# Six modulation pieces on GpSimd in place of TensorE, and first-layer products in halves

## The chip, the cores and the metric

The kernel runs on one core of one Trainium2 chip. The metric is the device time of one execution in microseconds; the median over the runs is what counts.

## The reference, cut to what matters

A token matrix x (256 tokens, 1024 features) and a context y (256 tokens) go through two mixing layers, and x then through a block with dilated attention, a convolution and a feed-forward part. The change touches the modulation of the first two layers, which comes from the vectors c and c_ctx alone, and the order of the products `h @ w_in` and of the attention in these layers:

```python
silu_c, silu_cc = jax.nn.silu(c), jax.nn.silu(c_ctx)
for l in range(DEPTH):                       # DEPTH = 2
    shift, scale, gate = jnp.split(silu_c @ w_mod[l] + b_mod[l], 3, axis=-1)
    shift_c, scale_c, gate_c = jnp.split(silu_cc @ w_mod[l] + b_mod[l], 3, axis=-1)
    hx = _rmsnorm(x, norm_g[l]) * (1.0 + scale[:, None, :]) + shift[:, None, :]
    hy = _rmsnorm(y, norm_g[l]) * (1.0 + scale_c) + shift_c
    fy, gy, qy, ky, vy, ay = _branches(hy, ...)   # products with w_in, Fourier, gating, q, k, v
    fx, gx, qx, kx, vx, ax = _branches(hx, ...)
    ox = _blocked_attention(qx, k_all, v_all) * jax.nn.silu(ax)
    x = x + gate[:, None, :] * (jnp.concatenate([fx, gx, ox], axis=-1) @ w_out[l])
```

`w_mod[l]` is 1024 x 3072. The kernel treats it as six pieces of 512 columns each, (l, n) with n = 0, 1 the shift, 2, 3 the scale and 4, 5 the gate.

## The kernel before, in words

Four engines each run a program of their own, written out by hand in the order in which it is carried out; semaphores tie them together, and nothing is scheduled by a planner. A wait blocks all that stands behind it on its engine. `tensor_program`, `scalar_program`, `vector_program` and `sync_program` walk through the same loops, and each must take its part of a step at the place that the others expect. Activations are kept transposed: features on the 128 partitions, tokens in the columns (512 in layer 0, context and x side by side; 256 in layer 1).

**Weights.** SyncE issues the weight chunks in a fixed order (`chunks` in `sync_program`, L2007) into a ring of four slots, `raw`, of 128x1024 each. A chunk may be issued when the chunk four before it has been taken from its slot. Nearly all are split for accuracy: ScalarE writes the rounded part `whi` (`highs`, L898), VectorE the rest `wlo` (`lows`, L1339), and TensorE makes three products per 128 rows, `whi*hh`, `whi*hl`, `wlo*hh` (`lin`, L350 to L355). `highs(key)` and `lows(key)` do not stop at the chunk that `key` needs. They go on to chunks further on, four ahead on ScalarE and three on VectorE, and only the generator `ahead` (L191) ends the run: it stops before a chunk i if one of the chunks from the present one to i - 4 is unsplit. So an engine can come to wait for a chunk that is needed much later.

**Modulation.** The four pieces (0, 2), (0, 0), (0, 3), (0, 1) are made at the start. The other pieces are made beside attention: `mod_g(l, n, g)` (L448) multiplies one unsplit raw chunk (two times 128 rows by 512 columns) with 32 columns of silu(c) on TensorE, four groups to a piece; ScalarE copies the 96x512 sums to `modrow` (`row`, L902), `mod_t` (L459) turns them with four transposes, and `bias` (L1363) on VectorE adds up and adds `b_mod`. In layer 0 the list `MODSTEPS0` gives one such step to each of 30 attention items: six pieces, (0, 4), (0, 5), (1, 2), (1, 3), (1, 0), (1, 1), of four groups and one transpose step each. In layer 1 the pieces (1, 4) and (1, 5) go the same way.

**Layer 0, in order** (`layer(0)`): the six first products (`FIRST`, L506 to L508), in two halves of their 1024 rows; the product for `gv` and the rotary key part (`lin_tm`, L420 to L422); the sums for the norms (L554, L558); k, v and q (L571, L573, L581); the Fourier part (L612 to L633); then attention. On ScalarE the copies out of PSUM after `lin_tm` (L1015) stand behind `highs` of the last chunk of that product. On VectorE the rotary tables (L1472, L1475) and the statistics (L1482 to L1352) stand behind `lows` of the same chunk.

**Attention.** 32 items in layer 0 (16 with 256 keys, 16 with 512), 16 in layer 1. At step i TensorE makes the scores of item i (L666), VectorE their maximum (L1673), ScalarE the exponentials (L1114), VectorE the division (L1680, L1682) of item i - 1, TensorE the transposes (L674) of item i - 2 and the values (L689) of item i - 4. The table `BESIDE` puts whole products between the scores and the transposes of some steps:

```python
BESIDE = ({0: ("agate", 0), 2: ("agate", 1), 4: ("agate", 2), 6: ("agate", 3), 9: ("ggate", 0), 12: ("gu", 0), 15: ("ggate", 1), 18: ("gu", 1), 20: ("gws", 0)},
          {0: ("agate", 0), 1: ("agate", 1), 3: ("agate", 2), 4: ("agate", 3), 6: ("gu", 1), 8: ("gws", 0)})
```

`LATE` says at which step the Fourier and spatial results are made ready for the last product, `wout`. GpSimd has no program: its four instructions are the framework's.

## Time and profile before

| | us |
|---|---|
| median of 3 runs | 981.33 (981.15 to 981.83) |
| the profiled execution, its own time | 986.22 |
| its span | 984.4 |
| mean granted TensorE clock | 0.965 |
| TensorE busy | 910.2 (92% of the span) |
| VectorE busy | 628.2 (64%) |
| ScalarE busy | 430.2 (44%) |
| GpSimd busy | 0.2 |

The span is the time between the first and the last instruction of the profiled execution. That execution was 4.9 us slower than the median of the runs, 1.8 us of it outside the span. A matmul's end is modelled in the profile, so rows of one engine overlap, and the step from one start to the next says more than the length of a row. TensorE's weight loads (PEld) lie beside its matmuls.

### The profile page before, as it was taken

The numbers are of one execution on the slowest core, as the hardware profiler recorded it, in microseconds if no ns is written. First come the engines' busy times: TensorE is split into PE (matmuls) and PEld (weight loads), VectorE is DVE, ScalarE is ACT, GpSimd is POOL, SyncE is SP. The second block draws the span as 40 slices with busy tenths as digits, with TensorE's granted clock in tenths as the row PEclk, the third lists the DMA queues.
The fourth block names the chain that finished last, engine by engine and source line by source line (L and its number), as shares of the span: only waits on it lengthen the run. The fifth ranks groups of instructions, "written<-read, shape, count | busy, mean of one in ns | idle before, by whom it ended". The sixth has DMA issues, their size and how long they took to land.

```text
span 984.4 us, 14348 instructions
## 1 busy us (share of the span) xinstructions
PE 910.2 (92%) x5858; PEld 746.5 (76%) x5858; DVE 628.2 (64%) x1242; ACT 430.2 (44%) x721; POOL 0.2 (0%) x4
## 2 busy tenths in 40 slices
PE   5899999999899799997999999898989799999994
PEld 1577666565478677764998888788888799999993
DVE  3454764644645749656679998976677755555554
ACT  3262143433533345345444444365543644444432
POOL 0000000000000000000000000000000000000000
PEclk9899999999799799999999999999999899999997
DMA  9560133434413133242556665442455256556531
GB/s 356 220 208 1 43 111 103 150 106 155 136 43 104 42 118 129 86 155 93 152 193 185 201 183 159 129 129 66 128 148 174 76 182 192 185 161 209 166 95 43
DMA packets 39954, 135.71 MB, mean 138 GB/s; under 512 B 4432, under 2 KB 5584, under 8 KB 39760
## 3 DMA queue, kind: packets, MB, share of 16 engines
q1 hardware_dynamic: 39024, 130.48, 40.8%
q10 hardware_dynamic: 864, 4.32, 1.2%
q8 instruction: 46, 0.75, 0.3%
q14 instruction: 20, 0.16, 0.1%
HBM read 133.73 MB, written 1.05 MB: 137 GB/s over the span
## 4 chain that ended last, share of the span: by engine, by line
PE 75%; DVE 16%; ACT 5%; DMA 3%; issue 1%; SPq 0%; ACTq 0%; DVEq 0%
PE ps L350 13%; PE ps L351 12%; PE ps L355 11%; PE ps L448 3%; PE ps L422 3%; PE ps L421 3%; PE ps L420 3%; PE ps L666 3%; DVE wlo L1339 3%; PE ps L689 2%; DMA raw<-wpack 2%; DVE AF L1800 2%; PE ps L353 2%; PE ps L868 1%; PE ps L506 1%; PE ps L674 1%
## 5 line engine op out<-in xcount | busy, mean ns | idle before, releaser
L350 PE MATMUL ps<-hh,whi 128*128 128x256 f32 (+1 forms) x1032 | 310.6, 301 | 3.7 <-DVE AF L1845 2.6
L351 PE MATMUL ps<-hl,whi 128*128 128x256 f32 (+1 forms) x1032 | 305.5, 296 | 0.0
L1339 DVE TENSOR_TENSOR wlo<-raw,whi 128x1024 fp32r<-128x1024 f32 (+3 forms) x206 | 234.1, 1150 | 62.7 <-ACT whi L898 62.5
L898 ACT ACTIVATE whi<-raw 128x1024 fp32r<-128x1024 f32 (+3 forms) x206 | 205.0, 997 | 151.2 <-DMA raw<-wpack 70.4
L355 PE MATMUL ps<-hh,wlo 128*128 128x256 f32 (+1 forms) x897 | 265.6, 296 | 0.0
L350 PEld LDWEIGHTS ps<-hh,whi 128*128 128x128 f32 x1032 | 198.9, 193 | 15.3 <-issue 9.0
L351 PEld LDWEIGHTS ps<-hl,whi 128*128 128x128 f32 x1032 | 199.1, 193 | 5.0 <-issue 0.7
L355 PEld LDWEIGHTS ps<-hh,wlo 128*128 128x128 f32 x897 | 173.1, 193 | 4.0
L420 PE MATMUL ps<-whi,hh 128*128 128x512 f32 (+1 forms) x192 | 70.7, 368 | 0.8 <-ACT wk L998 0.8
L421 PE MATMUL ps<-wlo,hh 128*128 128x512 f32 (+1 forms) x192 | 70.2, 366 | 0.0
L422 PE MATMUL ps<-whi,hl 128*128 128x512 f32 (+1 forms) x192 | 70.2, 366 | 0.0
L1114 ACT ACTIVATE AF<-ps,AF 128x512 f32<-128x512 f32 (+1 forms) x48 | 29.6, 617 | 86.9 <-DVE AF L1673 86.9
L1673 DVE TENSOR_REDUCE AF<-ps 128x1 f32<-128x512 f32 (+1 forms) x48 | 28.7, 598 | 37.0 <-PE ps L666 36.7
L1800 DVE SCALAR_TENSOR_TENSOR AF<-AF,cst 128x256 f32<-128x256 f32 x120 | 52.0, 483 | 0.4
L674 PEld LDWEIGHTS ps<-cst,AF 128*128 128x128 f32 x160 | 18.5, 147 | 42.2 <-DVE AF L1682 23.1
L666 PE MATMUL ps<-AF 96*128 96x512 f32 (+1 forms) x96 | 46.9, 571 | 2.3 <-DVE AF L1555 1.3
L420 PEld LDWEIGHTS ps<-whi,hh 128*128 128x128 f32 x192 | 36.0, 188 | 6.6 <-DVE wlo L1339 1.0
L422 PEld LDWEIGHTS ps<-whi,hl 128*128 128x128 f32 x192 | 36.0, 188 | 5.6
L421 PEld LDWEIGHTS ps<-wlo,hh 128*128 128x128 f32 x192 | 36.1, 188 | 5.5
L353 PE MATMUL ps<-hh,wlo 128*128 128x256 f32 (+1 forms) x135 | 39.7, 294 | 0.0
L1971 DVE TENSOR_TENSOR AF<-AF,ps 128x256 f32<-128x256 f32 x22 | 9.3, 421 | 46.9 <-PE ps L353 46.9
L674 PE MATMUL ps<-cst,AF 128*128 128x128 f32 x160 | 28.7, 296 | 11.3 <-DVE AF L1682 11.3
(254 smaller groups left out, 1275.9 us busy)
## 6 DMA issues: line engine op xcount, KB each, us to landing
raw<-wpack SPq DMA_DIRECT2D x196, 512.0 KB, 4.1
AF<-wmod SPq DMA_DIRECT2D x16, 512.0 KB, 10.3
raw<-wpack SPq DMA_DIRECT2D x16, 448.0 KB, 4.1
raw<-wpack SPq DMA_DIRECT2D x24, 256.0 KB, 2.8
XT<-xin SPq DMA_DIRECT2D x4, 512.0 KB, 6.1
raw<-wpack SPq DMA_DIRECT2D x4, 432.0 KB, 3.3
uq<-wuq ACTq DMA_DIRECT2D x2, 768.0 KB, 5.1
cst<-cpack ACTq DMA_DIRECT2D x1, 1093.0 KB, 7.9
```

The lines of the kernel that those rows point to most:

```text
L350: e.matmul(o, wh[:, b], xh(k), start=j == 0, stop=False, skip_group_check=True)
L351: e.matmul(o, wh[:, b], xl(k), start=False, stop=False, skip_group_check=True)
L353: e.matmul(o, wl[:, b], xh(k), start=False, stop=True, skip_group_check=True).then_inc(*M.up(key))
L355: e.matmul(o, wl[:, b], xh(k), start=False, stop=False, skip_group_check=True)
L420: e.matmul(o, xh(k)[:, ts], wh[:, b], start=k == 0, stop=False, skip_group_check=True)
L421: e.matmul(o, xh(k)[:, ts], wl[:, b], start=False, stop=False, skip_group_check=True)
L422: i = e.matmul(o, xl(k)[:, ts], wh[:, b], start=False, stop=k == KD - 1, skip_group_check=True)
L666: e.matmul(ps.ap(key, n), g.Q[0:96, t % 2, h, :], g.K[0:96, h, 0:n], start=True, stop=True, skip_group_check=True).then_inc(*M.up(key))
L674: n = e.transpose(ps.ap(key, P, j * P), g.Pb[:, o:o + P], C("ident"))
L898: e.activation(W.hi(i), W.raw(i), ACT.Copy).then_inc(*HI.up(j))
L1339: e.tensor_tensor(W.lo(i), W.raw(i), W.hi(i), ALU.subtract).then_inc(*LO.up(j))
L1800: e.scalar_tensor_tensor(out=g.CV[:, m, :], in0=g.U[:, m, j:j + 256], scalar=w, in1=g.CV[:, m, :], op0=ALU.mult, op1=ALU.add).then_inc(*V. ...
```

## The change

GpSimd gets a program, `gpsimd_program`. For each of the six pieces and each of the eight blocks k of 128 rows it takes a 128x512 block of `w_mod`, multiplies it by the two per-partition scalars silu(c_ctx)[k] and silu(c)[k], and adds both products to an accumulator of 128x1024. The first block of a piece has the two multiplications alone. That makes 48 block steps: 6 of two instructions and 42 of four. TensorE only sums the accumulator over the partitions, with eight matmuls against one column of ones (`mod_sum`), and `bias` reads that result with one instruction less. The four groups, the copy to `modrow` and the transposes of these six pieces are gone, and with them 24 unsplit chunks of the ring.

The blocks come by DMAs of 256 KB. The first 24 (`MFIRST`) are issued by SyncE, between the weight chunks, into three slots inside the tile `ag`; each from the fourth on waits until GpSimd is done with the block three before it. The other 24 are issued by ScalarE during attention (`MLOAD`), into the places of `modrow` and `ckv`. The sums stand at these places: (0, 4) before the product for `gv`, (0, 5) after the norm sums, (1, 2) before the second `kv_proj`, (1, 3) and (1, 0) at attention steps 13 and 24, (1, 1) before the seventh `wout` product. ScalarE's `agate` tanhs wait for GpSimd, since they write `ag`.

The products beside attention are split into two halves of 512 rows (`lin_first`, `lin_rest`), at two steps each, in both layers, and `LATE` moves from (22, 10) to (27, 14).

```diff
-MODS0 = ((0, 4), (0, 5), (1, 2), (1, 3), (1, 0), (1, 1))
+MODS = ((0, 4), (0, 5), (1, 2), (1, 3), (1, 0), (1, 1))
+MFIRST = 24
+MLOAD = {4 * n // 3: MFIRST + n for n in range(24)}
+MODS_AT = {13: (1, 3), 24: (1, 0)}
-LATE = (22, 10)
+LATE = (27, 14)
+BESIDE = (halves(*(("agate", m, 2 * m, 2 * m + 1) for m in range(4)), ("ggate", 0, 9, 11), ("gu", 0, 13, 15), ("ggate", 1, 17, 19), ("gu", 1, 21, 23), ("gws", 0, 25, 25)),
+          halves(*(("agate", m, 2 * m, 2 * m + 1) for m in range(4)), ("gu", 1, 9, 11), ("gws", 0, 12, 12)))
...
+    def mod_sum(l, n):
+        key = ("modT", l, n)
+        pe.wait_ge(G["mod", l, n], *ps.take(key))
+        acc = K.macc(MODS.index((l, n)))
+        for j in range(4):
+            for s in range(2):
+                i = e.matmul(ps.ap(key, 1, 2 * j + s), acc[:, 512 * s + P * j:512 * s + P * j + P], C("ones", 0, 1), start=True, stop=True, skip_group_check=True)
+        i.then_inc(*M.up(key))
...
+        def mod_load(j):
+            ac.wait_ge(G["w", j - 2] if j >= MFIRST + 2 else M["modT", 0, 1], M[l, "v", 3])
+            e.dma_start(K.mslot(j), K.wmodg[j]).then_inc(*K.mw_in[3 + j % 2].up(("in", j)))
...
+    def mods(a, b):
+        for j in range(a, b):
+            sp.wait_ge(G["w", j - 3] if j >= 3 else K.mm["mod", 0, 2])
+            e.dma_start(K.mslot(j), K.wmodg[j]).then_inc(*K.mw_in[j % 3].up(("in", j)))
...
-    chunks(6, len(W.plan))
+    chunks(6, 9)
+    mods(0, 3)
+    for i in range(6):
+        chunks(9 + i, 10 + i)
+        mods(3 + i, 4 + i)
+    mods(9, 11)
+    chunks(15, 16)
+    mods(11, 17)
+    chunks(16, 17)
+    mods(17, MFIRST)
+    chunks(17, len(W.plan))
...
+def gpsimd_program(K, e):
...
+    for p, a in enumerate(MODS):
...
+        for k in range(KD):
...
+            if k == 0:
+                e.tensor_scalar(o0, w, c0, None, ALU.mult, ALU.bypass).then_inc(*G.up(("p0", j)))
+                e.tensor_scalar(o1, w, c1, None, ALU.mult, ALU.bypass).then_inc(*G.up(("w", j)))
+            else:
+                e.tensor_scalar(tmp, w, c0, None, ALU.mult, ALU.bypass).then_inc(*G.up(("p0", j)))
+                e.tensor_scalar(w, w, c1, None, ALU.mult, ALU.bypass).then_inc(*G.up(("p1", j)))
+                po.wait_ge(G["p0", j])
+                e.tensor_tensor(o0, o0, tmp, ALU.add).then_inc(*G.up(("s0", j)))
+                po.wait_ge(G["p1", j])
+                e.tensor_tensor(o1, o1, w, ALU.add).then_inc(*G.up(("w", j)))
```

Three places show how the change moves instructions. The first is SyncE's queue, from the last early modulation load on, before the change (L2007 is a weight chunk; the rows are chunks 6 to 11, 12 and 13, 14, 15, and from 16 on):

```order
L1997 DMA AF<-wmod 128x1024 x4
L2007 DMA raw<-wpack 128x512 x6
L2007 DMA raw<-wpack 128x864 x2
L2007 DMA raw<-wpack 128x576
L2007 DMA raw<-wpack 128x512
L2007 DMA raw<-wpack 128x1024 x26
```

and with the change (L2064 is a weight chunk, L2071 a block for GpSimd), from chunk 13 on:

```order
L2064 DMA raw<-wpack 128x864
L2071 DMA AF<-wmodg 128x512
L2064 DMA raw<-wpack 128x576
L2071 DMA AF<-wmodg 128x512 x3
L2064 DMA raw<-wpack 128x512
L2071 DMA AF<-wmodg 128x512 x6
L2064 DMA raw<-wpack 128x1024
L2071 DMA AF<-wmodg 128x512 x7
L2064 DMA raw<-wpack 128x1024 x8
```

Chunk 16 (the second `fgate`) now stands behind blocks 11 to 16, and chunk 17 (`agate` 0), 18 and 19 behind blocks 17 to 23, the last of which waits for GpSimd's block step 20.

The second place is ScalarE around the copies after the `gv` product (L1015 before, L1050 now). Before:

```order
L898 ACTIVATE whi<-raw 128x1024 [waits raw_in0]
L974 ACTIVATE AF<-ps 128x512 [waits mm_done]
L898 ACTIVATE whi<-raw 128x1024 [waits raw_in2]
L1015 ACTIVATE AF<-ps 128x32 [waits mm_done]
L1016 ACTIVATE AF<-ps 128x256
```

and with the change:

```order
L933 ACTIVATE whi<-raw 128x1024 [waits raw_in0]
L1009 ACTIVATE AF<-ps 128x512 [waits mm_done]
L933 ACTIVATE whi<-raw 128x1024 [waits raw_in1]
L933 ACTIVATE whi<-raw 128x1024 [waits mm_done,raw_in2]
L1050 ACTIVATE AF<-ps 128x32 [waits mm_done]
L1051 ACTIVATE AF<-ps 128x256
```

Ahead of the copies stood chunks 16 and 18 (`fgate` 1 and `agate` 0), and chunk 17 was an unsplit modulation chunk. Now chunks 16, 17 and 18 stand there: `fgate` 1, `agate` 0 and `agate` 1.

The third is VectorE at the same point, ahead of the rotary tables (L1472 before, L1520 now). Before:

```order
L1339 TENSOR_TENSOR wlo<-raw,whi 128x576 [waits w_high]
L1339 TENSOR_TENSOR wlo<-raw,whi 128x1024 [waits w_high] x2
L1472 TENSOR_TENSOR rtab<-cst 128x64 [waits c1_in]
L1475 TENSOR_TENSOR rtab<-cst 128x2x8 x4
```

and with the change:

```order
L1382 TENSOR_TENSOR wlo<-raw,whi 128x576 [waits w_high]
L1382 TENSOR_TENSOR wlo<-raw,whi 128x1024 [waits w_high] x3
L1520 TENSOR_TENSOR rtab<-cst 128x64 [waits c1_in]
L1523 TENSOR_TENSOR rtab<-cst 128x2x8 x4
L1520 TENSOR_TENSOR rtab<-cst 128x64
L1523 TENSOR_TENSOR rtab<-cst 128x2x8 x4
L1413 TENSOR_TENSOR mod<-ps,cst 128x8 [waits mm_done]
L1532 TENSOR_SCALAR AF<-ps 128x4 [waits mm_done]
```

The splits of chunks 16, 17 and 18 now come ahead of the tables, of the bias of piece (0, 4) (L1413) and of the norm statistics (L1532).

## Rows read from the trace of the kernel before

**Rows 1.** The page, part 1: busy time, share of the span, instructions.

```profile
span 984.4 us, 14348 instructions
...
PE 910.2 (92%) x5858; PEld 746.5 (76%) x5858; DVE 628.2 (64%) x1242; ACT 430.2 (44%) x721; POOL 0.2 (0%) x4
```

**Rows 2.** Stretch: length, busy (x) of PE, PEld, DVE, ACT, POOL; clock; DMA.

```profile
128.00:276.00 148.00, 137.59 (x728) 82.94 (x728) 79.72 (x192) 63.52 (x136) 0.00 (x0) 0.95 0.39 127
```

**Rows 3.** Who waited for whom, 128 to 276 us: in total, times, longest.

```profile
PEld ps L674 <- DVE AF L1682: 14.3, 10, 3.4
```

**Rows 4.** Chain that ended last: start us, length us, what.

```profile
85.93 1.68 PE ps L554 x16
87.61 0.89 PE ps L558 x8
...
227.21 0.98 PE ps L448 x4
```

**Rows 5.** TensorE in order of time, 229 us: start, length, instruction.

```profile
229.48 0.49 PE L459 MATMUL ps<-cst,modrow 96*128 96x96 f32 x4
229.81 0.60 PE L674 MATMUL ps<-cst,AF 128*128 128x128 f32 x4
```

**Rows 6.** SyncE's queue, 49 to 52 us: start, length, DMA.

```profile
50.95 0.33 SPq L2007 DMA_DIRECT2D raw<-wpack  x1
```

**Rows 7.** The page, part 6: DMA issues, KB each, us to landing.

```profile
raw<-wpack SPq DMA_DIRECT2D x196, 512.0 KB, 4.1
...
raw<-wpack SPq DMA_DIRECT2D x24, 256.0 KB, 2.8
```

**Rows 8.** VectorE by line and shape, 128 to 276 us: busy, mean ns.

```profile
L1339 DVE TENSOR_TENSOR wlo<-raw,whi 128x1024 fp32r<-128x1024 f32 x10 | 12.2, 1225 | 21.0 <-ACT whi L898 21.0
...
L1682 DVE TENSOR_SCALAR AF<-AF 128x512 f32<-128x512 f32 x16 | 7.8, 487 | 0.6
```

**Rows 9.** Busy time by stretch, 54 to 90 us: VectorE's line L1339, then L1429.

```profile
54.00:90.00 36.00, 8.78 (x10) 0.99 0.40 136
...
54.00:90.00 36.00, 2.92 (x7) 0.99 0.40 136
```

**Rows 10.** GpSimd in order of time: the last of its four.

```profile
0.33 0.10 POOL L2171 MEMSET const-uint8-127<- 128x1 uint8 x1
```

**Rows 11.** ScalarE in order of time, 60 to 88 us.

```profile
74.75 1.06 ACT L898 ACTIVATE whi<-raw 128x1024 fp32r<-128x1024 f32 x1 [0.87 <-DMA raw<-wpack]
85.97 0.20 ACT L1015 ACTIVATE AF<-ps 128x32 f32<-128x32 f32 x1 [10.16 <-PE ps L422]
```

**Rows 12.** VectorE in order of time, 60 to 91 us.

```profile
76.98 0.22 DVE L1472 TENSOR_TENSOR rtab<-cst 128x64 f32<-128x64 f32 x1
...
77.59 0.43 DVE L1475 TENSOR_TENSOR rtab<-cst 128x16 f32<-128x16 f32 x4
88.54 0.16 DVE L1482 TENSOR_SCALAR AF<-ps 128x4 f32<-128x4 f32 x1 [10.52 <-PE ps L558]
...
90.01 0.17 DVE L1352 SCALAR_TENSOR_TENSOR AF<-AF 128x8 f32<-128x8 f32 x1
```

**Rows 13.** VectorE in order of time, 110 to 116 us.

```profile
112.93 2.48 DVE L1515 COPY AF<-ps 128x512 f32<-128x512 f32 x4
```

**Rows 14.** TensorE in order of time, 88 to 116 us.

```profile
88.36 1.10 PE L571 MATMUL ps<-AF 128*128 128x512 f32 x2
...
114.83 0.59 PE L632 MATMUL ps<-cst,AF 128*128 128x256 f32 x2
```

**Rows 15.** TensorE in order of time, 260 to 276 us.

```profile
260.32 1.11 PE L674 MATMUL ps<-cst,AF 128*128 128x128 f32 x4 [2.49 <-DVE AF L1682]
262.06 1.97 PE L689 MATMUL ps<-AF 128*64 128x128 f32 x16 [0.63 <-ACT AF L1121]
...
273.75 0.66 PE L674 MATMUL ps<-cst,AF 128*128 128x128 f32 x4 [0.94 <-DVE AF L1682]
274.45 1.09 PE L689 MATMUL ps<-AF 128*64 128x128 f32 x16
```

More of the change, by code:

```diff
@@ L298, in mod_order, with halves @@
     return out
[L301 to L303 removed]
+LATE = (27, 14)
 def out_step(l, t):
     return max(8 * (t - 2 * l) + 10, LATE[l] + 2 + t % 2)
[L312 to L313 removed]
+def halves(*places):
+    out = {}
+    for nm, m, a, b in places:
+        out[a] = (nm, m, 0)
+        out[b] = (nm, m, 1)
+    return out
+BESIDE = (halves(*(("agate", m, 2 * m, 2 * m + 1) for m in range(4)), ("ggate", 0, 9, 11), ("gu", 0, 13, 15), ("ggate", 1, 17, 19), ("gu", 1, 21, 23), ("gws", 0, 25, 25)),
+          halves(*(("agate", m, 2 * m, 2 * m + 1) for m in range(4)), ("gu", 1, 9, 11), ("gws", 0, 12, 12)))
 def fills(i):
@@ L544, in layer @@
             lin_many([spec("cq", 0), spec("cq", 1), spec("ckv", 0, True), spec("fin", 0), spec("fin", 1)], ht)
+        if l == 0:
+            mod_sum(0, 4)
         st = (l, "st")
@@ L560, in layer @@
         ps.drop(st)
+        if l == 0:
+            mod_sum(0, 5)
         if l == 1:
@@ L643, in layer @@
                 heads_T("q", 0, 1, y)
+            mod_sum(1, 2)
             kv_proj(1)
@@ L697, in layer @@
         mt = lambda k: V[l, "mix", k]
-        steps = list(MODSTEPS0) if l == 0 else mod_order(((1, 4), (1, 5)))
+        steps = mod_order(MODS1) if l else []
+        half = None
         for i in range(ni + 3):
@@ L711, in layer @@
                 heads_T("q", 1, 0, 1)
+            if l == 0 and i in MODS_AT:
+                mod_sum(*MODS_AT[i])
             if steps:
@@ L731, in layer @@
         for m in range(len(begun), KD):
+            if l == 0 and m == 6:
+                mod_sum(1, 1)
             lin((l, "wout", m), "w_out", l, (P * m, P), range(KD), xh, xl, N, mt)
@@ L980, in gate @@
             highs(key)
-            ac.wait_ge(M[key], *bar)
+            ac.wait_ge(M[key], G["w", min(MFIRST - 3 + m, MFIRST - 1)] if l == 0 and nm == "agate" else None, *bar)
             e.activation(dst, ps.ap(key, N), ACT.Tanh, scale=0.5).then_inc(*A.up(key))
@@ L1132, in layer @@
                 exps(i)
-            if i - 1 in BESIDE[l]:
-                beside(*BESIDE[l][i - 1])
+            if l == 0 and i in MLOAD:
+                mod_load(MLOAD[i])
+            if i - 1 in BESIDE[l] and (BESIDE[l][i - 1][2] or BESIDE[l][i - 1][0] == "gws"):
+                beside(*BESIDE[l][i - 1][:2])
             if l == 0 and i == 0:
@@ L1156, in layer @@
             if i in BESIDE[l] and BESIDE[l][i][0] != "gws":
-                highs((l, *BESIDE[l][i]))
+                highs((l, *BESIDE[l][i][:2]))
             for m in range(2):
@@ L1477, in layer @@
         V.mark((l, "tab"))
+        if l == 0:
+            bias(0, 4)
         st = ps.ap((l, "st"), 8)
@@ L1486, in layer @@
         V.mark((l, "stat"))
+        if l == 0:
+            bias(0, 5)
         n = 4 * len(tiles)
@@ L1619, in layer @@
                 heads_T("q", 0, 1, y)
+            bias(1, 2)
             kv_take(1, 0, M[l, "kT", 0, 1, 4])
@@ L1694, in layer @@
         ni = len(items)
-        steps = list(MODSTEPS0) if l == 0 else mod_order(((1, 4), (1, 5)))
+        steps = mod_order(MODS1) if l else []
         def mod_step(what, a, g_):
@@ L1707, in layer @@
                 norm(i - 1)
-            if i - 1 in BESIDE[l]:
-                beside(*BESIDE[l][i - 1])
+            if i - 1 in BESIDE[l] and (BESIDE[l][i - 1][2] or BESIDE[l][i - 1][0] == "gws"):
+                beside(*BESIDE[l][i - 1][:2])
             if l == 0:
@@ L1738, in layer @@
                     heads_T("q", 1, 0, 1, M[l, "s", 15])
+            if l == 0 and i in MODS_AT:
+                bias(*MODS_AT[i])
             if steps:
@@ L1743, in layer @@
             if i in BESIDE[l] and BESIDE[l][i][0] != "gws":
-                lows((l, *BESIDE[l][i]))
+                lows((l, *BESIDE[l][i][:2]))
             for m in range(2):
@@ L1759, in layer @@
             key = (l, "wout", m)
+            if l == 0 and m == 6:
+                bias(1, 1)
             lows(key, 4 if l == 0 and m == KD - 1 else 3)
@@ L2114, in _ @@
             vector_program(K, e)
+        @block.gpsimd
+        def _(e):
+            gpsimd_program(K, e)
     return plan
```

81 lines of the change are left out of this document (55 added, 26 removed).

## The prediction

> **What bounds the kernel now.** I read the page's first part, then stretches, waits, the chain, and last the order of single instructions. The page shows TensorE busy for 92% of the span and GpSimd with nothing to do [rows 1]. That alone would make any work moved from TensorE to GpSimd a gain. The stretch of layer 0's attention says the same: from 128 to 276 us TensorE is busy for 137.6 of 148 us, VectorE for 79.7 and ScalarE for 63.5, at a granted clock of 0.95 [rows 2]. The largest true wait of TensorE there is for VectorE's divisions, 14.3 us of idle weight loads [rows 3], most of it after 245 us. So before that point a microsecond taken off TensorE is a microsecond of the kernel.
>
> **What leaves TensorE.** A modulation group is one link of 0.98 us in the chain [rows 4]; 24 of them go: 23.5 us. Four transposes hold TensorE for 0.33 us, from 229.48 to the next start at 229.81 [rows 5]; six sets go: 2.0 us. Together 25.5 us.
>
> **What comes to TensorE.** `mod_sum` is eight matmuls of a 128x128 operand on one column. The norm sums have just this form: eight of them took 1.68 us [rows 4]. Six sums are 10.1 us. Two of them, (0, 4) and (0, 5), stand before or inside the wait that I find below and cost nothing; that cover goes if the wait goes, and they then cost 3.4 us. The other four cost 6.7 us. Net on TensorE: 25.5 - 6.7 = 18.8 us gained. The halves issue the same matmuls, and the ring has lost the 24 modulation chunks, so I count the split, `LATE` and the 12 fewer small VectorE and ScalarE instructions at nothing. What hides them is TensorE's own full queue up to 245 us; if VectorE became late there, they would show.
>
> **What GpSimd takes.** Its only rows are 128x1 memsets of 0.10 us [rows 10], so the price of its instructions is not in the trace, and I bound it by VectorE's. VectorE takes 0.49 us for 128x512 with one input, and 1.22 us for 128x1024 with two [rows 8]. Low end: GpSimd is as fast as VectorE, 0.49 us for the multiplication and 0.69 for the addition (the 128x512 splits: nearly all of the ten in 54 to 90 us are of that kind or in proportion, 8.8 us [rows 9]). A full block step is then 2.36 us. High end: 0.69 for the multiplication and 1.22 for the addition, so 3.82 us. I take 0.59 and 1.22, a step of 3.62 us, near the high end, since nothing shows GpSimd to keep VectorE's pace. A first step of a piece, two multiplications, is 1.18 us. The Trainium skill (GPSIMD Engine Reference, "Elementwise — side-by-side cycle accounting") gives 4497 ns for an fp32 `tensor_tensor` of 2048 columns and 1.03 cycles per element at 1.2 GHz for short bodies: an estimate by it is about 1.1 and 0.45 us, a step of 3.1 us, and with that the sum below would be 9 us lower. No row here shows it.
>
> **When GpSimd gets where.** Blocks 0 to 2 are loaded early. Block 3 is issued behind weight chunk 9, which leaves at 50.95 us [rows 6]; 0.33 us more for the issue and 2.8 us for 256 KB [rows 7] put it in place at 54.1 us. From there GpSimd has no gap, for three slots and two steps of 3.62 us cover a landing. It ends block 15 at 54.1 + 12 x 3.62 + 1.18 = 98.7, and block 20 at 98.7 + 1.18 + 4 x 3.62 = 114.4 us.
>
> **The wait that the change adds.** This is the term that decides. SyncE issues chunk 17 only behind block 23, and block 23 waits for GpSimd's block 20: 114.4 us. Behind that chunk hang two queues that need something else. ScalarE rounds chunks 17 and 18 before its copies out of PSUM, and VectorE splits both before the tables, the statistics and all that follows; this is the look-ahead of `highs` and `lows`, which the unsplit chunk 17 used to keep shorter. Before, ScalarE had its last chunk of that group at 74.75 us and waited for TensorE until 85.97, with ten microseconds to spare [rows 11]. Now: 0.7 us for two issues, 4.1 us for 512 KB [rows 7], two roundings of 1.06 us [rows 11], one split of 1.22 us [rows 8], tables of 1.0 us (76.98 to 78.0), a bias of 0.2, and statistics of 1.6 us (88.54 to 90.18) [rows 12]. That is 10.9 us, and the statistics are ready at 125.3 instead of 90.2 us: 35.1 us late. TensorE cannot run on meanwhile: k, v and q are scaled by these statistics, and PSUM banks are full of what ScalarE has not fetched. Further down VectorE's chain reached its Fourier copies at 112.93 and TensorE wanted the first at 114.83 [rows 13, 14]; the first of four copies in 2.48 us ends at 113.5, so 1.3 us of the delay is lost in that gap. The shift at the start of attention is 33.8 us. GpSimd's block 15 (98.7) and block 23 (125.3) are then no wait of their own.
>
> **The clock.** After an idle of 2.5 us at 260 us, four transposes took 1.11 us instead of 0.66 and a set of values 1.97 instead of 1.09 [rows 15]: the granted clock had fallen to its lower level, 1.2 GHz. An idle of 25 us should do the same. I take 3 us for it, some seven microseconds of work at 1.75 times its length; the ends are 0 and 6.
>
> **Sum.** 33.8 + 3 - 18.8 = 18.0 us slower. The profiled execution took 986.2 us, 4.9 more than the median of 981.3. 986.2 + 18.0 = 1004.2, and on the scale of the median 999.3 us.
>
> **Bounds of the forecast.** With the low step of 2.36 us block 20 ends at 93.8, the shift is 13.2, and the sum is -2.6 us (978.7 on the median's scale). With the high step block 20 ends at 118.0, the shift is 37.4 and the sum 21.6 us. With a step from 3.1, the middle of the two ends, to 3.82 us and the clock's ends, the forecast's own range is 988 to 1006.
>
> **Rival one: the two engines hold each other up.** VectorE and GpSimd both read and write SBUF, and nothing in a trace without GpSimd work tells what that costs. At the far end each waits for the other. From 54 to 90 us VectorE has 11.7 us of instructions with two SBUF inputs, ten of L1339 and seven of L1429 [rows 9], nearly all before 78 us, while GpSimd works on blocks 3 to 9. If they exclude each other, block 20 comes 12 us later, at 126. Then blocks 21 to 23 still run (12 instructions) beside VectorE's chain of small ones, and each can hold one up by up to its own 0.6 to 1.2 us: I take 8 us. In attention a division that waits for half an instruction of GpSimd costs some 0.4 us wherever TensorE waits for it, the last dozen items: 5 us. Together 25 us on top: 1024 us. For it speaks that both take 128-partition operands from one memory; against it, that VectorE's splits, run beside a ScalarE busy for 43% of that stretch, keep a mean of 1225 ns [rows 2, 8]. The Trainium skill (SBUF — State Buffer, "Who interferes with whom") has this as a rule: VectorE in a two-port mode or with two SBUF inputs, and GpSimd, take one pair of ports as an exclusive lock. No row here can show it.
>
> **Rival two: faster.** If GpSimd keeps VectorE's pace, block 20 ends at 94, chunk 17 lands at 98, and the shift of 13.2 us is less than the 18.8 us gained. The point from which this decides is a shift of 16 us, block 20 before 97 us, a step below 2.5 us. It gives 975 to 980 us; with the clock at no cost, 976.
>
> **Rival three: the gain in attention is not there.** Without the groups, attention may run at the pace of VectorE and ScalarE, which already hold TensorE up late in it [rows 3], or ScalarE may wait for GpSimd ahead of a load and hold back the exponentials. The groups after 245 us and a wait at some of the 22 such loads would take back 6 to 10 us: 1005 to 1009.
>
> **How the numbers follow.** The forecast has 0.5, the mutual hold 0.29, the fast GpSimd 0.12, the lost gain 0.09. A measurement of this kernel can tell about 0.2%, 2 us, from no change. All but the fast GpSimd are slower; of that case I give 0.09 to faster and 0.03 to no change, and 0.02 of the forecast's low edge goes to no change. The range takes in both ends of the step and the mutual hold: 978 to 1024. The predicted time is 999.
>
> **What would show it.** Right: GpSimd's starts repeat about every 3.6 us; ScalarE waits some 35 us for chunk 17 (raw) before its copies at L1050, and VectorE about as long at L1382 ahead of the tables; TensorE is idle between about 90 and 121 us; attention of layer 0 lasts about 126 instead of 148 us. Wrong: chunk 17 lands before 100 us, or TensorE has no gap over 10 us there. Mutual hold would show in VectorE's 128x512 splits longer than 0.69 us between 54 and 62 us.

## The result and the profile after: 1071 us against 981

The changed kernel takes 1071.2 us (median of 4 runs, 1071.2 to 1073.4), the kernel before 981.2 beside it. The ratio is 1.092, 95% interval 1.090 to 1.094. The forecast was 999, its range ended at 1024. The sign and the mechanism were right, the size was not.

The page's first part of the kernel after, to be held against [rows 1]:

```profile
PE 909.4 (85%) x5834; PEld 765.0 (71%) x5834; DVE 658.1 (61%) x1236; ACT 427.5 (40%) x715; POOL 273.9 (26%) x184
```

TensorE has as much to do as before, in a longer span. GpSimd works for 274 us. VectorE has six instructions fewer and 30 us more: they got longer.

The stretches of the kernel after (columns as in [rows 2]):

```profile
54.00:90.00 36.00, 22.55 (x85) 17.81 (x84) 11.03 (x12) 9.71 (x18) 35.83 (x24) 0.76 0.43 138
90.00:128.00 38.00, 17.34 (x123) 17.25 (x122) 2.00 (x1) 1.54 (x2) 38.00 (x29) 0.68 0.21 63
128.00:175.00 47.00, 13.40 (x33) 7.76 (x34) 14.38 (x30) 7.04 (x14) 43.13 (x31) 0.53 0.19 56
209.00:357.00 148.00, 119.84 (x613) 86.17 (x611) 89.96 (x172) 52.93 (x118) 128.42 (x82) 0.86 0.23 72
```

From 54 to 171 us GpSimd alone is full. The three other engines are each busy for less than half of 54 to 175 us (TensorE 53.3 of 121), and the granted clock falls to 0.53. The last line is layer 0's attention over the same length as in [rows 2]: TensorE is busy for 120 of 148 us instead of 138.

SyncE's issues in time (start, length, line). L2064 issues weight chunks, L2071 blocks; a long row is a series whose waits lie in it:

```profile
90.18 28.11 SPq L2071 DMA_DIRECT2D AF<-wmodg  x6
118.34 0.43 SPq L2064 DMA_DIRECT2D raw<-wpack  x1
123.50 31.38 SPq L2071 DMA_DIRECT2D AF<-wmodg  x7
154.92 112.06 SPq L2064 DMA_DIRECT2D raw<-wpack  x12
```

Chunk 16 leaves at 118.34 and chunk 17 at 154.92, behind GpSimd's blocks 13 and 20. The two queues of the prediction hang on them. ScalarE and VectorE in the same stretch (in brackets the idle time before, and what ended it):

```profile
122.12 1.06 ACT L933 ACTIVATE whi<-raw 128x1024 fp32r<-128x1024 f32 x1 [44.04 <-DMA raw<-wpack]
158.68 1.06 ACT L933 ACTIVATE whi<-raw 128x1024 fp32r<-128x1024 f32 x1 [35.01 <-DMA raw<-wpack]
```

```profile
123.21 2.00 DVE L1382 TENSOR_TENSOR wlo<-raw,whi 128x1024 fp32r<-128x1024 f32 x1 [44.57 <-ACT whi L933]
159.76 3.67 DVE L1382 TENSOR_TENSOR wlo<-raw,whi 128x1024 fp32r<-128x1024 f32 x2 [34.55 <-ACT whi L933]
168.84 1.28 DVE L1395 SCALAR_TENSOR_TENSOR AF<-AF 128x8 f32<-128x8 f32 x1
170.12 1.20 DVE L1545 TENSOR_REDUCE AF<-AF 128x16 f32<-128x1024 f32 x1
```

The statistics end at 170.1; in the kernel before they ended at 90.2 [rows 12]. Attention starts at 209.0, before at 128.7. TensorE's rows there:

```profile
86.93 3.57 PE L488 MATMUL ps<-cst,AF 128*128 128x1 f32 x16 [9.58 <-POOL AF L2124]
129.15 3.57 PE L488 MATMUL ps<-cst,AF 128*128 128x1 f32 x16 [21.81 <-POOL AF L2124]
167.08 2.07 PE L600 MATMUL ps<-AF 128*128 128x512 f32 x2 [32.45 <-DVE mod L1413]
208.96 0.60 PE L694 MATMUL ps<-AF 96*128 96x256 f32 x2
```

Behind these idles a piece's sum takes 3.57 us; the granted clock over both rows is 0.50. The sum of (1, 1), later on, is a row of 1.84 at full clock (the norm sums, of the same form, count 1.68 in the chain [rows 4]):

```profile
400.19 1.84 PE L488 MATMUL ps<-cst,AF 128*128 128x1 f32 x16
```

The sign that the prediction named for a mutual hold, a 128x512 split longer than 0.69 us between 54 and 62 us, is there:

```profile
55.20 1.77 DVE L1382 TENSOR_TENSOR wlo<-raw,whi 128x512 fp32r<-128x512 f32 x1
```

What GpSimd costs: one of its groups (busy us, mean ns of one), then one step, block 21, in time:

```profile
L2120 POOL TENSOR_SCALAR AF<-AF,c 128x512 f32<-128x512 f32 x33 | 58.5, 1773 | 0.0
```

```profile
154.48 1.58 POOL L2119 TENSOR_SCALAR AF<-AF,c 128x512 f32<-128x512 f32 x1
156.02 1.58 POOL L2120 TENSOR_SCALAR AF<-AF,c 128x512 f32<-128x512 f32 x1
157.55 1.28 POOL L2122 TENSOR_TENSOR AF<-AF 128x512 f32<-128x512 f32 x1
158.77 1.29 POOL L2124 TENSOR_TENSOR AF<-AF 128x512 f32<-128x512 f32 x1
160.02 1.59 POOL L2119 TENSOR_SCALAR AF<-AF,c 128x512 f32<-128x512 f32 x1
```

With VectorE idle a block step is 160.02 - 154.48 = 5.54 us. The prediction took 3.62 and ended its range at 3.82. The product with one input is the dearer of the two: 1.54 us from start to start against 1.23.

### The profile page after: what moved, and what is told of

Read it like the earlier page. It is cut to its first block, busy times and chain, and to the rows that moved or that the text cites. A ratio compares the mean times of both kernels' runs of the same rounds, so it can differ in the third digit from the quotient of the medians.

```text
span 1071.5 us, 14537 instructions
## 1 busy us (share of the span) xinstructions
PE 909.4 (85%) x5834; PEld 765.0 (71%) x5834; DVE 658.1 (61%) x1236; ACT 427.5 (40%) x715; POOL 273.9 (26%) x184
## 4 chain that ended last, share of the span: by engine, by line
PE 62%; POOL 14%; DVE 14%; issue 4%; ACT 3%; DMA 3%; SPq 0%; ACTq 0%; DVEq 0%; POOLq 0%
PE ps L363 10%; PE ps L364 10%; PE ps L368 9%; POOL AF L2120 4%; POOL AF L2122 3%; POOL AF L2119 3%; PE ps L433 3%; PE ps L435 3%; PE ps L434 3%; DVE wlo L1382 2%; POOL acc L2119 2%; DVE AF L1857 2%; PE ps L608 1%; PE ps L366 1%; PE ps L618 1%
## 5 line engine op out<-in xcount | busy, mean ns | idle before, releaser
L1382 DVE TENSOR_TENSOR wlo<-raw,whi 128x1024 fp32r<-128x1024 f32 (+3 forms) x206 | 238.9, 1174 | 122.2 <-ACT whi L933 121.9
L363 PE MATMUL ps<-hh,whi 128*128 128x256 f32 (+1 forms) x928 | 271.3, 292 | 3.7 <-DVE AF L1902 2.6
L364 PE MATMUL ps<-hl,whi 128*128 128x256 f32 (+1 forms) x928 | 267.6, 288 | 0.0
L368 PE MATMUL ps<-hh,wlo 128*128 128x256 f32 (+1 forms) x806 | 232.5, 288 | 0.0
L363 PEld LDWEIGHTS ps<-hh,whi 128*128 128x128 f32 x928 | 177.8, 192 | 9.2 <-issue 5.1
L364 PEld LDWEIGHTS ps<-hl,whi 128*128 128x128 f32 x928 | 177.8, 192 | 2.6 <-issue 0.7
L368 PEld LDWEIGHTS ps<-hh,wlo 128*128 128x128 f32 x806 | 154.4, 192 | 1.7
L2120 POOL TENSOR_SCALAR AF<-AF,c 128x512 f32<-128x512 f32 x33 | 58.5, 1773 | 0.0
L702 PEld LDWEIGHTS ps<-cst,AF 128*128 128x128 f32 x160 | 20.9, 156 | 45.8 <-DVE AF L1735 34.1
L694 PE MATMUL ps<-AF 96*128 96x512 f32 (+1 forms) x96 | 47.7, 580 | 0.9 <-ACT AF L1081 0.9
L2124 POOL TENSOR_TENSOR AF<-AF 128x512 f32<-128x512 f32 x33 | 44.1, 1336 | 0.0
L488 PE MATMUL ps<-cst,AF 128*128 128x1 f32 x96 | 16.1, 297 | 31.4 <-POOL AF L2124 31.4
```

The source lines that it names most:

```text
L363: e.matmul(o, wh[:, b], xh(k), start=j == 0, stop=False, skip_group_check=True)
L364: e.matmul(o, wh[:, b], xl(k), start=False, stop=False, skip_group_check=True)
L368: e.matmul(o, wl[:, b], xh(k), start=False, stop=False, skip_group_check=True)
L702: n = e.transpose(ps.ap(key, P, j * P), g.Pb[:, o:o + P], C("ident"))
L1382: e.tensor_tensor(W.lo(i), W.raw(i), W.hi(i), ALU.subtract).then_inc(*LO.up(j))
L2120: e.tensor_scalar(w, w, c1, None, ALU.mult, ALU.bypass).then_inc(*G.up(("p1", j)))
```

## The experiments

All times are medians; each is compared with the kernel before in the same batch (978.5 to 981.3 us, single runs of it 974 to 986). The last two columns are read from TensorE's rows of the one profiled execution: the start of layer 0's first score matmul (L666 in before and e5 to e7, L676 in e4, L694 in the others), and the time from there to the start of the scores of that layer's last item.

| Kernel | us | ratio to before [95%] | first score at | first to last |
|---|---|---|---|---|
| before | 981.2 | 1 | 128.7 | 142.6 |
| after | 1071.2 | 1.092 [1.090, 1.094] | 209.0 | 146.0 |
| e1 all steps narrow | 976.1 | 0.996 [0.993, 0.998] | 138.5 | 121.6 |
| e2 chunks first | 1047.7 | 1.068 [1.065, 1.072] | 184.5 | 143.9 |
| e3 products whole | 1063.4 | 1.085 [1.081, 1.088] | 210.2 | 136.9 |
| e4 halves alone, on before | 984.2 | 1.004 [1.001, 1.006] | 130.4 | 145.0 |
| e5 before, GpSimd multiplies beside it | 1020.6 | 1.043 [1.037, 1.049] | 158.4 | 148.1 |
| e6 before, GpSimd memsets beside it | 979.9 | 1.000 [0.996, 1.004] | 126.1 | 142.2 |
| e7 before, four GpSimd forms beside it | 996.7 | 1.018 [1.008, 1.027] | 142.6 | 141.4 |
| e8 narrow ahead of attention | 1000.1 | 1.021 [1.015, 1.027] | 136.9 | 142.7 |
| e9 e8 and GpSimd's own loads | 1006.4 | 1.026 [1.019, 1.033] | 140.1 | 147.8 |
| e10 products in the two-input form | 1056.5 | 1.078 [1.073, 1.083] | 195.9 | 143.5 |
| e11 all of GpSimd's cost away | 969.2 | 0.989 [0.985, 0.993] | 135.3 | 121.7 |
| e12 e8 with memsets in attention | 982.5 | 1.002 [0.999, 1.005] | 139.6 | 128.5 |
| e13 memsets in all steps | 1041.7 | 1.062 [1.058, 1.066] | 195.6 | 125.9 |
| e14 three mends together | 1038.9 | 1.059 [1.056, 1.063] | 185.2 | 137.5 |

### Is it GpSimd's time at all? (e1)

```diff
+                n_ = slice(0, 16)
-                e.tensor_scalar(tmp, w, c0, None, ALU.mult, ALU.bypass).then_inc(*G.up(("p0", j)))
+                e.tensor_scalar(tmp[:, n_], w[:, n_], c0, None, ALU.mult, ALU.bypass).then_inc(*G.up(("p0", j)))
...
```

> Of the changed kernel's block steps after the first of each piece, GpSimd computes only 16 of the 512 columns; every instruction, wait, DMA and sum stays, so the modulation is wrong and only GpSimd's own time is taken out. Theory (the loss is GpSimd's pace, handed on by waits): GpSimd is never late, chunk 17 lands before 80 us, and the time is that of before less what TensorE was relieved of: 981 - 25.5 + 10.1, that is 964 to 970. Rival (the loss lies in the order, the halves, the DMAs or the extra waits themselves): over 990.

976.1 us: with GpSimd's long steps gone, 95 us go, five more than the change had cost. So the loss is GpSimd's time. The result is 6 us above the expected band. Chunk 17 did not land before 80 us as expected: it is issued at 87.82, still behind all 24 blocks. Attention starts 9.8 us later than in the kernel before and is 21.0 us shorter from first to last score.

### The order of the chunks (e2), the halves (e3, e4)

```diff
-    mods(9, 11)
-    chunks(15, 16)
-    mods(11, 17)
-    chunks(16, 17)
-    mods(17, MFIRST)
-    chunks(17, len(W.plan))
+    chunks(15, 19)
+    mods(9, MFIRST)
+    chunks(19, len(W.plan))
```

> The changed kernel with SyncE's queue reordered alone: weight chunks 15 to 18 are issued ahead of blocks 9 to 23, so neither look-ahead waits for GpSimd. Theory: the 34.5 us in which ScalarE and VectorE wait for chunk 17 go, but TensorE then stands at its own wait for the sum (0, 5), block 15, until 129 us, and for (1, 2), block 23, until about 171 us; attention starts near 176 instead of 209, and the time is 1071 - 33 = 1038, within 8. Rival (chunk 17 is the only cause): a shift near zero, time under 1000. Rival (mutual hold is the cause): no change, 1065 to 1072.

1047.7, 24 us less than the changed kernel, 1.7 above the expected band. Attention starts at 184.5, where 176 was expected. The wait for chunk 17 is gone, and the sum of piece (0, 5) is late next; TensorE's row of it in e2:

```profile
131.52 3.57 PE L488 MATMUL ps<-cst,AF 128*128 128x1 f32 x16 [21.36 <-POOL AF L2121]
```

```diff
-    BESIDE: every product of attention in halves, LATE = (27, 14)
+    BESIDE: whole products at the steps of the kernel before, LATE = (22, 10)
```

> The changed kernel with the products beside attention whole again, at the steps of before, and LATE as before; GpSimd as in the change. Theory (halves are worth nothing while GpSimd sets the pace): 1066 to 1076. Rival (the halves carry part of the loss through PSUM or weight loads): under 1062.

> The kernel before with the halves and LATE of the change alone, no GpSimd. Theory: same matmuls, TensorE full: within 2 us of 981. Rival (halves smooth attention): 974 to 979. Rival (halves cost): over 984.

In the changed kernel the halves with their `LATE` cost 8 us (1071.2 to 1063.4), between the two expectations; alone on the kernel before they cost about 3 us (ratio 1.004), at the edge of "halves cost". The prediction had counted them at nothing. The gain of e3 lies in attention, 136.9 us against 146.0. Split and `LATE` were not separated.

### The mutual hold by itself (e5, e6, e7)

```diff
+        @block.gpsimd
+        def _(e):
...
+            for i in range(420):
+                e.wait_ge(sg, n)
+                e.tensor_tensor(a, a, b, ALU.mult).then_inc(sg, 1)
+                n += 1
```

> The kernel before, and on GpSimd 420 two-input multiplications of 128x244 in a scratch of its own, one behind the other, for which nobody waits. Work and output are the reference's. Theory of the mutual hold (VectorE and GpSimd hold each other up where both read and write the on-chip memory): VectorE's rows between 20 and 300 us get longer, the 128x512 splits (0.49 and 0.69 us alone) by at least half on the mean, and the kernel by 10 to 50 us though nobody waits for GpSimd. Rival (the two don't touch; what was held up in the changed kernel was held by its own waits): VectorE's rows keep their lengths within 5%, and the time is 981 within 3 us.

> As the run with the two-input multiplications, but with 420 memsets of 128x244, which write and read nothing. If the mutual hold comes of GpSimd's reading, this kernel takes 981 within 3 us with VectorE's rows unchanged; if any GpSimd work holds VectorE, it is as slow per GpSimd operation as the run with the multiplications.

Nobody waits for GpSimd in either. The multiplications cost 42 us, the memsets nothing. The multiplications run until 382 us, the shorter memsets only until 155. VectorE's groups of the kernel before, of e5 and of e6, over the whole span, but L1429 from 50 to 128 us:

```profile
L1682 DVE TENSOR_SCALAR AF<-AF 128x512 f32<-128x512 f32 x32 | 15.6, 487 | 1.1
L1339 DVE TENSOR_TENSOR wlo<-raw,whi 128x512 fp32r<-128x512 f32 x20 | 13.6, 688 | 1.3 <-ACT whi L898 1.2
L1429 DVE SCALAR_TENSOR_TENSOR hl<-AF,mod,hh 128x256 fp32r<-128x256 f32 x8 | 3.5, 482 | 0.0
```

```profile
L1682 DVE TENSOR_SCALAR AF<-AF 128x512 f32<-128x512 f32 x32 | 19.6, 612 | 1.1
L1339 DVE TENSOR_TENSOR wlo<-raw,whi 128x512 fp32r<-128x512 f32 x20 | 18.6, 936 | 1.4 <-ACT whi L898 1.4
L1673 DVE TENSOR_REDUCE AF<-ps 128x1 f32<-128x512 f32 x32 | 21.9, 686 | 19.3 <-PE ps L666 19.3
...
L1429 DVE SCALAR_TENSOR_TENSOR hl<-AF,mod,hh 128x256 fp32r<-128x256 f32 x8 | 7.0, 914 | 0.0
```

```profile
L1339 DVE TENSOR_TENSOR wlo<-raw,whi 128x512 fp32r<-128x512 f32 x20 | 13.6, 687 | 3.3 <-ACT whi L898 3.2
...
L1429 DVE SCALAR_TENSOR_TENSOR hl<-AF,mod,hh 128x256 fp32r<-128x256 f32 x8 | 3.5, 479 | 0.0
```

Beside the multiplications VectorE's instructions with two on-chip inputs take 914 instead of 482 ns. The means over the whole span hide a part of it. Between 20 and 320 us the 128x512 splits take 1103 instead of 689 ns, and the fast one-input division (L1682) 737 instead of 487. The reduction that reads PSUM keeps 686 ns. In e6 all the 128x512 divisions come after the last memset and say nothing; five 128x256 divisions came before it and took 435 ns on the mean instead of 354. The Trainium skill (SBUF — State Buffer, "Who interferes with whom") has this as an exclusive lock between GpSimd and VectorE in a two-port mode, or with two SBUF inputs. With two inputs, it says, VectorE contends only with a GpSimd instruction that reads SBUF. The rows agree: beside memsets the two-input splits keep 687 ns. Most of the 42 us come ahead of attention (158.4 against 128.7).

The pace of each form was e7's question:

> The kernel before, and on GpSimd ten rounds of ten memsets, ten one-input products by an immediate number, ten one-input products by a number for each partition, and ten two-input products, all 128x244 in a scratch of its own, for which nobody waits. It is for the pace of each form. Theory (the number for each partition makes the one-input form slow): immediate 0.35 us and per-partition 0.8 us start to start. Rival one (the one-input form is slow in both): both 0.75 to 0.85 us, above the two-input form at 0.6 to 0.7. Rival two (1.54 us of the changed kernel was contention with VectorE): both one-input forms under the two-input form where VectorE is idle.

Shortest, median and longest of 100 each, all 128x244 (memset; immediate; per-partition number; two-input):

```profile
L2125 POOL MEMSET gx<- x100: 301/301/544, 4.0 to 306.4; 128x244 f32 x100
L2129 POOL TENSOR_SCALAR gx<-gx x100: 817/819/2056, 7.8 to 317.2; 128x244 f32<-128x244 f32 x100
L2133 POOL TENSOR_SCALAR gx<-gx,c x100: 892/894/2498, 16.8 to 330.1; 128x244 f32<-128x244 f32 x100
L2137 POOL TENSOR_TENSOR gx<-gx x100: 697/709/1769, 26.8 to 340.6; 128x244 f32<-128x244 f32 x100
```

Rival one: the one-input form is slow with either number, already in the shortest rows, so it is no contention. These are lengths of rows; each instruction waits for the one before, and from start to start they repeat every 0.36, 0.90, 0.99 and 0.79 us.

### A cheaper product (e10)

```diff
-            c0, c1 = K.c32[:, 32 * k:32 * k + 1], K.c32[:, 32 * k + 1:32 * k + 2]
+            c0, c1 = (K.c32[:, 32 * k + s:32 * k + s + 1].broadcast_to([P, 512]) for s in range(2))
-                e.tensor_scalar(tmp, w, c0, None, ALU.mult, ALU.bypass).then_inc(*G.up(("p0", j)))
+                e.tensor_tensor(tmp, w, c0, ALU.mult).then_inc(*G.up(("p0", j)))
...
```

> The changed kernel with GpSimd's products written in the two-input form (the number for each partition read again and again as second operand): a block step should take four times 1.27 instead of twice 1.57 and twice 1.27 us, 0.6 less, and the result is the same. If the time ahead of attention is GpSimd's 20 blocks one behind the other, statistics and attention come 11 to 14 us earlier, and with a little of the same in attention the kernel takes 1050 to 1060. Rival (GpSimd's price was not what set the place of attention, but the hold-ups beside VectorE and the order of the chunks): 1066 or more. Rival two (the repeated operand costs GpSimd as much or more): 1071 or above.

1056.5, in the band. The product with a repeated operand costs less than guessed; block 9 of e10:

```profile
86.20 1.04 POOL L2119 TENSOR_TENSOR AF<-AF,c 128x512 f32<-128x512 f32 x1
...
88.20 1.28 POOL L2122 TENSOR_TENSOR AF<-AF 128x512 f32<-128x512 f32 x1
89.44 1.28 POOL L2124 TENSOR_TENSOR AF<-AF 128x512 f32<-128x512 f32 x1
90.68 1.04 POOL L2119 TENSOR_TENSOR AF<-AF,c 128x512 f32<-128x512 f32 x1
```

A step is 4.48 us. Attention starts 13.1 us earlier and the kernel is 14.7 shorter, so the time does go by GpSimd's steps ahead of attention.

### What GpSimd costs in attention (e8, e9, e12, e13)

```diff
-                n_ = slice(0, 16)
+                n_ = slice(0, 16 if first else 512)
```

> The changed kernel in which the steps of blocks 0 to 23 (before attention) behind the first of each piece compute 16 of 512 columns, and those of blocks 24 to 47 (in attention) all 512: the modulation of the first three pieces is wrong. Theory (80 us of the loss come ahead of attention and some 10 to 17 in it, where ScalarE's loads wait for GpSimd): attention starts at 138 us as with all steps narrow (976.1 us), and the kernel takes 986 to 995. Rival (the pace in attention hardly matters, since the loads wait only because everything is late): 976 to 979. Rival two (attention is paced by GpSimd's 24 blocks of 5.5 us and loses more once it starts early): 1000 or more.

1000.1, 5 us above the theory's band and at the very edge of rival two's: the wide steps of attention cost 24 us once everything else is early (e1 to e8). Two causes were left: ScalarE's exponentials behind its waits for GpSimd, or the mutual hold. First the loads were taken off ScalarE:

```diff
-            if l == 0 and i in MLOAD:
-                mod_load(MLOAD[i])
...
+            for jj in ((MFIRST, MFIRST + 1) if j == MFIRST else (j + 1,) if j > MFIRST and j + 1 < 2 * MFIRST else ()):
+                po.wait_ge(G["w", jj - 2] if jj >= MFIRST + 2 else M["modT", 0, 1], M[0, "v", 3])
+                e.dma_start(K.mslot(jj), K.wmodg[jj]).then_inc(*K.mw_in[3 + jj % 2].up(("in", jj)))
```

> The changed kernel with the steps of blocks 0 to 23 narrow (as in the run at 1000 us), in which GpSimd itself issues the loads of blocks 24 to 47, each as its slot comes free, and ScalarE none: ScalarE's exponentials no longer stand behind a wait for GpSimd (16.5 us in 6 waits there between 128 and 300 us). The modulation of the first three pieces is wrong. Theory A (of the 24 us that the wide steps in attention cost, most is ScalarE's waiting for GpSimd): 978 to 986. Theory B (most is the mutual hold of VectorE and GpSimd, which stays): 988 to 1002, with VectorE's 128x512 splits in attention still near 0.78 us instead of 0.49.

1006.4, above both bands: nothing won. But VectorE's sixteen 128x512 divisions were at 1163 ns there, longer than in e8 (841), and each load was a new GpSimd row of 0.59 us, so a second thing had changed and the run does not settle it. The next one does:

```diff
-                e.tensor_scalar(tmp, w, c0, None, ALU.mult, ALU.bypass).then_inc(*G.up(("p0", j)))
...
+                for dst, key in ((tmp, "p0"), (w, "p1"), (o0, "s0"), (o1, "w")):
+                    n = 3 if key == "p0" else 2
+                    for r in range(n):
+                        po.wait_ge(G.now())
+                        e.memset(dst, 1.0).then_inc(*G.up((key, j)) if r == n - 1 else G.up())
```

> The changed kernel with the steps of blocks 0 to 23 narrow, as in the run at 1000 us, and in blocks 24 to 47 the four operations of a step replaced by nine memsets of 128x512 (one at about 0.6 us, worked out from 0.30 us for 128x244): GpSimd is as long at each block, ScalarE's loads wait for it as before, but GpSimd reads nothing. The modulation is wrong. Theory (the 24 us of the wide steps in attention are the mutual hold): 976 to 982. Rival (they are ScalarE's waiting for GpSimd, and the run with GpSimd's own loads lost what it gained there through its DMA issues): 992 or more. Between: both.

982.5, half a microsecond above the theory's band. With GpSimd nearly as long at each block and ScalarE still waiting for it (14.3 us in 5 waits, 16.5 in 6 in e8), but nothing read, 18 of the 24 us are gone. From first to last score attention takes 128.5 us instead of 142.7. VectorE from 128 to 300 us, in e12 and then in e8:

```profile
L1382 DVE TENSOR_TENSOR wlo<-raw,whi 128x1024 fp32r<-128x1024 f32 x12 | 14.5, 1216 | 2.0 <-ACT whi L933 2.0
L1735 DVE TENSOR_SCALAR AF<-AF 128x512 f32<-128x512 f32 x16 | 10.8, 676 | 0.6
L1643 DVE TENSOR_TENSOR AF<-AF,rtab 128x64 f32<-128x64 f32 x16 | 2.5, 219 | 0.0
```

```profile
L1382 DVE TENSOR_TENSOR wlo<-raw,whi 128x1024 fp32r<-128x1024 f32 x10 | 13.4, 1349 | 1.4 <-ACT whi L933 1.4
L1735 DVE TENSOR_SCALAR AF<-AF 128x512 f32<-128x512 f32 x16 | 13.4, 841 | 0.6
L1643 DVE TENSOR_TENSOR AF<-AF,rtab 128x64 f32<-128x64 f32 x16 | 7.7, 542 | 0.0
```

The two-input instructions are free of the memsets: the rotations (L1643) take 219 ns beside them and 542 beside the readings. The division is not free: 676 ns for 128x512 (516 in e1) and 505 for 128x256 (355 in e1; 371 in e8). Over all 32 divisions memsets cost nearly as much as readings, 18.9 us of busy time against 19.3, and 13.9 in e1. So the 18 us do not come from the division. VectorE's instructions in that attention add up to 86.0 us in e1, 90.9 in e12 and 104.7 in e8, and nearly all of the 13.8 between the last two lie in two-input instructions, 5.2 of them in the rotations. The splits count for little: of the eight in e8 between 128 and 276 us seven took 1.22 us and one 2.28. e12 is no exact price, since it still has some hold and its steps are a little shorter.

The same memsets in every step of the changed kernel:

> The changed kernel with nine memsets in the place of the four operations in every step behind the first of a piece, ahead of attention too: GpSimd's pace of about 5.5 us a block is kept, its reading is gone. The modulation is wrong. Theory (ahead of attention the 80 us are pace and order alone, in attention the mutual hold costs 10 to 20): attention starts at 200 to 209 us instead of 209, and the kernel takes 1042 to 1060. Rival (the mutual hold is a large part ahead of attention too): attention starts ahead of 195 us and the time is under 1040. Rival two (no hold matters anywhere): 1066 or more.

1041.7, 29.5 less than the changed kernel, just under the theory's band and above the rival's. Attention starts at 195.6, between theory and rival, and takes 125.9 us instead of 146.0. Some 4 us of these 13.4 are the memsets' slightly quicker step (37.04 us for seven of them, 5.29 each), the rest is put down to time in which GpSimd and VectorE held each other; one execution shows it.

### All of the gain, and all mends

e11 takes narrow steps, whole products and the chunk order of e2 together; its diff is theirs.

> All of GpSimd's cost taken away, the whole gain left: steps behind the first of each piece narrow (modulation wrong), the first layers' products whole at the places of the kernel before, chunks 15 to 18 issued ahead of blocks 9 to 23. TensorE does the reference's work without the modulation's six pieces. The prediction's term for this was a gain of 18.8 us: 962 against 981. Theory (the term was right and only the price of GpSimd wrong): 960 to 967. Rival (TensorE's 25.5 us were largely cover for its waits for VectorE and ScalarE, which come out as idle time): 970 to 978.

969.2, 2.2 us above the first band and 0.8 below the rival's. From first to last score attention is 20.9 us shorter than before, and it begins 6.6 us later. Three of the six sums now stand ahead of it, rows of 1.84, 2.58 and 1.84 us, which is nearly all of that.

e14 has the chunk order of e2, the whole products of e3 and the product form of e10, and computes all of it.

> The changed kernel with three mends together: products whole at the places of the kernel before (8 us alone), chunks 15 to 18 issued ahead of blocks 9 to 23 (24 us alone), GpSimd's products in the two-input form (15 us alone). The work and the output are the reference's. If the mends add up, 1024 (1018 to 1032), still slower than the kernel before. Rival (with the chunks first GpSimd is no longer ahead of anything until its second sum, and the mends overlap): 1033 to 1045. Rival two (the rest falls away once GpSimd is in time): under 1000.

1038.9, the first rival: the mends do not add up. Attention starts at 185.2, no earlier than with the chunks alone. The sum of (0, 5) comes 10.4 us earlier than in e2 (121.15 against 131.52), and VectorE's chain of small dependent instructions behind it gives the time back. It runs while GpSimd still works (piece (1, 2), until about 157.5 us). Rows of e14:

```profile
154.19 0.97 DVE L1393 TENSOR_TENSOR AF<-AF 128x16 f32<-128x16 f32 x1
...
162.23 0.17 DVE L1393 TENSOR_TENSOR AF<-AF 128x16 f32<-128x16 f32 x1
```

The same instruction takes 0.97 us beside GpSimd and 0.17 us without: each waits out about one instruction of GpSimd. But in e2 the same chain ran beside a working GpSimd too, and it was mostly quick. Two rows of VectorE and one of GpSimd from e2:

```profile
154.63 0.17 DVE L1393 SCALAR_TENSOR_TENSOR AF<-AF 128x16 f32<-128x16 f32 x1
154.84 0.47 DVE L1395 SCALAR_TENSOR_TENSOR AF<-AF 128x16 f32<-128x16 f32 x1
```

```profile
154.59 1.57 POOL L2117 TENSOR_SCALAR AF<-AF,c 128x512 f32<-128x512 f32 x1
```

The difference lies, by these rows, in the form of GpSimd's products; no run took it by itself. Of VectorE's small instructions (up to 16 columns) with two on-chip inputs that started under a GpSimd `tensor_tensor`, 30 of 34 took over 0.3 us in e14; under a `tensor_scalar` it was 8 of 39 in e2. A `tensor_scalar` holds them only in its first 0.7 us: the second row ends 0.72 us after the product began, and three more in e2 end 0.70 to 0.71 after theirs. So the cheaper two-input product of e10 is also the one that holds VectorE all the time. TensorE pays for it with this wait in e14, which is 4.86 us in e2:

```profile
166.62 1.22 PE L659 MATMUL ps<-cst,AF 128*128 128x256 f32 x2 [15.35 <-DVE AF L1569]
```

No version that computes everything came below the kernel before. By these runs none with a smaller share on GpSimd should: a piece saves at most 20.9 / 6 = 3.5 us, and three pieces in attention cost 24 us, 8 each. That is worked out, not run.

## Why the prediction was wrong in size

**What bounds the kernel, and what leaves TensorE: right.** The prediction had attention at 126 instead of 148 us. Without GpSimd's cost it is 20.9 us shorter (e11). Over the whole kernel the forecast's gain was 18.8 us, or 15.4 with the two early sums paid for, as in e11; e11 has 1.1% (0.7 to 1.5), about 11, since attention begins 6.6 us later. The price of a sum holds at full clock.

**The wait that the change adds: right in its place.** Chunk 17 is issued behind block 20, ScalarE waits 35.0 us for it, VectorE 34.6, and the statistics are late. What stands in front of it was overlooked: chunk 16 behind block 13, with a wait of 44.0 us of its own. It comes ahead of chunk 17 and adds nothing to the sum.

**The step that failed is "What GpSimd takes": 3.62 us for a block step, high end 3.82.** It was 5.53. The bound came from VectorE, on the reasoning that the high end was already VectorE's 1024-column time for a GpSimd addition of 512 columns. For the addition that was right (1.22 taken, 1.23 measured). The product was taken at 0.59 and measured at 1.54, 2.6 times as long; one input was assumed cheaper than two, as on VectorE, and on GpSimd it is dearer. The estimate by the Trainium skill (GPSIMD Engine Reference, "Elementwise — side-by-side cycle accounting"), 0.45 us, was further off; for the addition its 1.1 us is near the 1.23 measured. Between block 3 and the end of block 20 lie 16 full and 2 first steps: 16 x 1.91 + 2 x 1.90 = 34.4 us more than forecast. Another 3.9 went by up to the issue of chunk 17, 3.5 of it in which GpSimd was held up or idle. Block 3 began 2.3 late, and behind block 20 came 15.2 us instead of 10.9 up to the statistics, since VectorE's splits, tables and small instructions there were themselves held (rows at 159.76 and 168.84). Together 44.9: statistics 79.9 us late instead of 35.1.

**Rival one, the mutual hold, is real and was mis-sized as an addition to the forecast.** It was priced at 25 us with 0.29. In attention GpSimd's reading costs about 18 us (e8 against e12, ratios 1.021 and 1.002), where the prediction gave the whole hold 5. A division that waits for half an instruction wherever TensorE waits for it left out the rotations (L1643, 542 ns in e8 and 245 in e1) and all the chains. And it should not have been a rival: it is no alternative to the slow step but comes on top.

**Rival three, ScalarE's waits for GpSimd: 6.5 us at most.** e12 against e1 gives 0.66% or 6.5 us, and that holds what memsets do to the division as well, 5.0 us of VectorE's time; how much is left for ScalarE's waits was not separated. The prediction had 6 to 10.

**The halves, `LATE`: not nothing.** They cost 8 us in the changed kernel, 3 alone. **Sums (0, 4) and (0, 5):** hidden, as forecast, with the chunks late; with the chunks first, (0, 5) is the wait (e2).

**The sum again**, by spans of the profiled executions, 1071.5 against 984.4: 87.1 us lost, 80.3 of them in the later start of attention (forecast 33.8) and 6.8 after it. For what follows the start the forecast had -15.8 (clock 3 less gain 18.8). The same difference, span less that of before less the later start, is -20.5 in e1, -10.9 in e12 and +7.2 in e8: the gain, then 9.5 for GpSimd's pace and what a memset holds, then 18.2 for its reading. e8 and the changed kernel (+6.8) agree. By the medians instead of single spans the four are -15.0, -9.8, +13.3 and +9.7, so each step is uncertain by some 5 us. The 3 us of the clock do not show: from the statistics to attention it is 38.9 us against 38.5 before, and 1.8 of that is a sum. What stays open is the split of the start's delay into pace and hold: e13 puts the hold at about 9 us, from one execution.

## What to carry to other kernels

An idle engine is not a free one: ask what its instructions cost on that engine, and whose port they take while they run. If no row of the trace has the instruction on that engine, the other engine's time is no bound; let the range reach twice beyond it. A form that is cheaper on the idle engine can hold its neighbour longer. And a load that waits for the slow engine must not stand in a queue ahead of loads that others need.
